# Experts' up projections with one 512-column moving operand, and most of the choice's one-hot sets under the experts

## The reference, cut to what matters

```python
def expert_choice_moe(h, lp):
    b, t, dm = h.shape
    cap = EC_CAPACITY * t // N_EXPERTS                      # 256
    affinity = jax.nn.softmax((h @ lp['router']).astype(jnp.float32), axis=-1)
    gate, idx = lax.top_k(jnp.swapaxes(affinity, 1, 2), cap)
    xs = jax.vmap(lambda hb, ib: hb[ib])(h, idx)
    hid = (jax.nn.silu(jnp.einsum('becd,edf->becf', xs, lp['moe_w1']))
           * jnp.einsum('becd,edf->becf', xs, lp['moe_w3']))
    y = jnp.einsum('becf,efd->becd', hid, lp['moe_w2']) * gate[..., None].astype(h.dtype)
    return jax.vmap(lambda yb, ib: jnp.zeros((t, dm), y.dtype).at[ib.reshape(-1)].add(yb.reshape(-1, dm)))(y, idx)
```

## Time and profile before

| | us |
|---|---|
| median of 3 runs | 4239.88 (4237.48 to 4244.39) |
| the profiled execution, its own time | 4230.22 |
| its span | 4228.4 |
| mean granted clock of TensorE, share of full | 0.935 |

### The profile page before, as it was taken

How to read it: one execution, slowest core, us unless ns; L and a number is a source line. 1 busy time by engine, 2 the same in 40 slices (tenths; PEclk the granted TensorE clock), 3 DMA queues, 4 the chain that set the end, 5 groups by cost and what they waited for, 6 DMA issues and landing times. The chain is left out here.

```text
span 4228.4 us, 114308 instructions
## 1 busy us (share of the span) xinstructions
PE 3605.5 (85%) x50045; PEld 3209.7 (76%) x50045; DVE 2429.1 (57%) x4363; ACT 1873.2 (44%) x3274; POOL 1295.8 (31%) x1262
## 2 busy tenths in 40 slices
PE   5799999999677777777777588798299999999997
PEld 2678888888577777777777588675199999999987
DVE  3246676620057676667766655433856666666666
ACT  3246665531145555555555544233044444444454
POOL 2223333321155555555554145101110201010202
PEclk8899999999889999999999889898599999999999
DMA  5235555532333333333332367342156767676787
GB/s 176 66 124 178 180 179 172 171 120 72 103 81 85 87 91 80 88 89 80 93 86 62 122 179 229 104 159 100 61 185 199 217 201 218 201 215 204 223 289 224
DMA packets 565269, 612.66 MB, mean 145 GB/s; under 512 B 66018, under 2 KB 469284, under 8 KB 563748
## 3 DMA queue, kind: packets, MB, share of 16 engines
q1 hardware_dynamic: 515620, 493.82, 37.9%
q0 software_dynamic: 22688, 80.75, 6.5%
q10 hardware_dynamic: 26464, 30.77, 2.4%
HBM read 443.62 MB, written 161.50 MB: 143 GB/s over the span
## 5 line engine op out<-in xcount | busy, mean ns | idle before, releaser
L424 DVE TENSOR_TENSOR moe_w_lo<-moe_w_lo_whole,moe_w_hi 128x2048 fp32r<-128x2048 f32 x254 | 446.6, 1758 | 281.7 <-ACT moe_w_hi L625 195.6
L559 PE MATMUL moe_h<-moe_xt_hi,moe_w_hi 128*128 128x256 f32 x2048 | 583.2, 285 | 6.6 <-DVE moe_w_lo L424 3.3
L559 PE MATMUL moe_h<-moe_xt_lo,moe_w_hi 128*128 128x256 f32 x2048 | 580.6, 283 | 0.0
L559 PE MATMUL moe_h<-moe_xt_hi,moe_w_lo 128*128 128x256 f32 x2048 | 580.5, 283 | 0.0
L1878 PE MATMUL inward_pp<-u_u_hi,inward_w_hi 128*128 128x512 f32 (+1 forms) x1360 | 527.1, 388 | 19.9 <-POOL inward_w_lo L2038 19.9
L1878 PE MATMUL inward_pp<-u_u_lo,inward_w_hi 128*128 128x512 f32 (+1 forms) x1360 | 515.5, 379 | 0.0
L1878 PE MATMUL inward_pp<-u_u_hi,inward_w_lo 128*128 128x512 f32 (+1 forms) x1360 | 515.3, 379 | 0.0
L559 PEld LDWEIGHTS moe_h<-moe_xt_hi,moe_w_hi 128*128 128x128 f32 x2048 | 393.7, 192 | 20.3 <-DVE moe_w_lo L424 8.8
L559 PEld LDWEIGHTS moe_h<-moe_xt_lo,moe_w_hi 128*128 128x128 f32 x2048 | 393.8, 192 | 3.6
L559 PEld LDWEIGHTS moe_h<-moe_xt_hi,moe_w_lo 128*128 128x128 f32 x2048 | 393.8, 192 | 0.0
L481 POOL DMA_INDIRECT scratch_x<-moe_ys,moe_who x30 | 88.2, 2941 | 843.9 <-DVE moe_ys L710 727.0
(11 more groups left out here) (395 smaller groups left out, 9868.7 us busy)
## 6 DMA issues: line engine op xcount, KB each, us to landing
moe_w_lo_whole<-in_moe_w SPq DMA_DIRECT2D x384, 512.0 KB, 5.4
scratch_ops<-inward_ops SPq DMA_DIRECT2D x72, 514.0 KB, 3.8
scan_over<-scratch_ops SPq DMA_DIRECT2D x72, 512.0 KB, 10.1
inward_w_lo_whole<-in_w_in SPq DMA_DIRECT2D x38, 512.0 KB, 4.6
scan_aq<-scratch_ops SPq DMA_DIRECT2D x36, 516.0 KB, 5.2
scratch_gates<-inward_out SPq DMA_DIRECT2D x64, 256.0 KB, 2.1
all_late<-in_w_mod POOLq DMA_DIRECT2D x32, 512.0 KB, 4.7
rest_modsum<-scratch_gates SPq DMA_DIRECT2D x64, 256.0 KB, 3.9
```

The costliest lines, as they stand in the source:

```text
L424: return nc.vector.tensor_tensor(x_lo, x, x_hi.bitcast(F32), ALU.subtract)
L559: mm = nc.tensor.matmul(hb[ft % 2][m][:, 0:CAP], w_, x_, start=(k == 0 and part == 0), stop=(k == KD - 1 and part == 2))
```

## The change

1. The experts' rows lie upper part and rest beside each other (`xt_parts`), so that one matmul of 512 columns with the same weights does upper by upper into the first half of a PSUM bank and upper by rest into the second half; rest by upper stays a matmul of 256 columns into the first half. Per slice 32 matmuls in place of 48.
2. The halves are added by VectorE: two `tensor_reduce` over pairs that lie 256 elements apart (steps hs0 and hs1), out of PSUM into `sl` and `hid`. Silu waits for hs0 and works in place in SBUF; `hid` then multiplies in SBUF. TensorE's `turn` waits for hs1.
3. In `choose` only the one-hot sets of experts 0 to 2 are left (`EARLY` = 3). The first weights' rests and the first rows' rests go from GpSimd to VectorE. The transposes of the first rows come after set 1.
4. The sets 3 to 15 are made in `experts`: expert e makes set e + 3 in slices 1 to 6 (3, 3, 3, 3, 2 and 2 tiles), at the end of VectorE's part of the slice. TensorE multiplies set e + 2 in slice 0 of expert e (1 to 13) between the first two `h` (`rows_of`), into bank `yb[0]`, after q3 of the expert before. VectorE collects it at the end of slice 0, and `down(0)` waits for that. GpSimd takes token numbers from `idxf`.
5. The tiles of `choose` share memory with the final norm's ring `x`.

```diff
-            pool.wait_ge(s_hi, 2)
-            pool.tensor_tensor(w13_lo[:, 0], w13[:, 0], w13_hi[:, 0].bitcast(F32), ALU.subtract).then_inc(s_lo, 1)
-            pool.tensor_tensor(w2_lo[:, 0], w2[:, 0], w2_hi[:, 0].bitcast(F32), ALU.subtract).then_inc(s_lo, 1)
...
-            for e in range(E_NUM):
+            def compare(e):
                 if e >= 2:
                     dve.wait_ge(s_mm, e - 1)
                 for k in range(NT):
                     at = (k // 2) * E_NUM + e
                     ins = dve.tensor_scalar(oh[:, e % 2, k, :], slots[:, :], slot[:, k % 2, at:at + 1], None, ALU.is_equal)
                 ins.then_inc(s_oh, 1)
-                if e:
-                    collect(e - 1)
-            collect(E_NUM - 1)
...
+            compare(0)
+            dve.wait_ge(s_hi, 2)
+            dve.tensor_tensor(w13_lo[:, 0], w13[:, 0], w13_hi[:, 0].bitcast(F32), ALU.subtract).then_inc(s_lo, 1)
+            collect(0)
+            compare(1)
+            dve.tensor_tensor(w2_lo[:, 0], w2[:, 0], w2_hi[:, 0].bitcast(F32), ALU.subtract).then_inc(s_lo, 1)
+            compare(2)
+            collect(1)
+            for q in range(4):
+                lower_rows(q)
+            collect(2)
...
-        xt, xt_lo = n.sb_both("xt_lo", [P, 2, KD, CAP])
-        xt_hi = n.sb("xt_hi", [P, 2, KD, CAP], F32R)
+        xt_whole, xt_part = n.sb_both("xt_parts", [P, 2, KD, 2, CAP])
+        xt, xt_hi, xt_lo = xt_whole[:, :, :, 1, :], xt_part[:, :, :, 0, :], xt_part[:, :, :, 1, :]
...
+        COMPARE = {1: range(0, 3), 2: range(3, 6), 3: range(6, 9), 4: range(9, 12), 5: range(12, 14), 6: range(14, 16)}
...
                         if ft == 0:
-
                             DV.wait(pe, f"{w}q3", j) if u else None
+                            if 1 <= 2 * i + u <= E_NUM - EARLY:
+                                pe.wait_ge(s_out, 2 * (2 * i + u))
...
+                    def rows_of(e):
+                        pe.wait_ge(s_oh, e - EARLY + 1)
+                        DV.wait(pe, f"{w}q3", j)
+                        for h in range(2):
+                            for k in range(NT):
+                                mm = nc.tensor.matmul(yb[0][:, 5 * h:5 * h + 5], oh[:, e % 2, k, h * P:(h + 1) * P], parts[:, k, e, :],
+                                                      start=(k == 0), stop=(k == NT - 1))
+                        mm.then_inc(s_listed, 1)
...
-                                xhi, xlo = xt_hi[:, u, k, :], xt_lo[:, u, k, :]
-                                for part, (w_, x_) in enumerate(((whi, xhi), (whi, xlo), (wlo, xhi))):
-                                    mm = nc.tensor.matmul(hb[ft % 2][m][:, 0:CAP], w_, x_, start=(k == 0 and part == 0),
-                                                          stop=(k == KD - 1 and part == 2))
+                                both = xt_part[:, u, k, :, :].rearrange("p a c -> p (a c)")
+                                if k == 0:
+                                    nc.tensor.matmul(hb[ft % 2][m][:, :], whi, both, start=True, stop=False)
+                                mm = nc.tensor.matmul(hb[ft % 2][m][:, 0:CAP], wlo, xt_hi[:, u, k, :], start=False, stop=False)
+                                if k:
+                                    mm = nc.tensor.matmul(hb[ft % 2][m][:, :], whi, both, start=False, stop=(k == KD - 1))
...
-                                DV.wait(pe, f"{u}hid{FT - 2 + part}", i)
+                                DV.wait(pe, f"{u}hs1{FT - 2 + part}", i)
                                 PE.did(f"{u}x{part}", turn(1 - u, part))
                         if ft:
                             down(ft - 1)
+                        elif 1 <= 2 * i + u <= E_NUM - EARLY:
+                            rows_of(2 * i + u + EARLY - 1)
...
-                        PE.wait(act, f"{u}h{ft}", i)
-
-                        DV.wait(act, f"{u}hid{ft - 2}" if ft >= 2 else f"{w}hid{ft + 6}", i if ft >= 2 else j)
-                        ins = act.activation(sl[:, ft % 2, :], hb[ft % 2][0][:, 0:CAP], ACT.Silu)
+                        DV.wait(act, f"{u}hs0{ft}", i)
+                        ins = act.activation(sl[:, ft % 2, :], sl[:, ft % 2, :], ACT.Silu)
...
+                        PE.wait(dve, f"{u}h{ft}", i)
+                        PE.wait(dve, f"{u}y{ft - 2}" if ft >= 2 else f"{w}y{ft + 6}", i if ft >= 2 else j)
+                        for m, to_ in enumerate((sl[:, ft % 2, :], whole)):
+                            ins = dve.tensor_reduce(to_, hb[ft % 2][m][:, :].rearrange("p (a c) -> p c a", a=2), AX_X, ALU.add)
...
+                        if ft == 0 and 1 <= e <= E_NUM - EARLY:
+                            collect(e + EARLY - 1)
+                        if ft in COMPARE and e < E_NUM - EARLY:
+                            compare(e + EARLY, COMPARE[ft])
```

117 lines of the change are left out of this document (66 added, 51 removed).

## The result

| | before | after |
|---|---|---|
| median of the comparison's 4 runs each, us | 4241.46 | 4207.35 (4197.89 to 4211.94) |
| the profiled execution, its own time, us | 4230.22 | 4211.72 |
| its span, us | 4228.4 | 4209.9 |

The ratio of the times is 0.9923, 95% interval 0.9907 to 0.994. The forecast was 4203.4 us, a gain of 36.5; the medians moved by 34.1. The profiled execution of after lies 4 us above its own median.

What follows compares the result with a forecast made beforehand. TensorE was taken to bound the experts, with VectorE's chain setting its start at an expert's end. Terms -42.4 - 17.3 + 11.7 + 12.4 - 2.9 + 2.0 = -36.5 us gave 4203.4 us, range 4190 to 4229.

Steps and rivals of the forecast that it cites:

- The choice, -36.2 and -6.2: Ahead of the experts: first set to first h falls from 59.6 to 23.4 us; GpSimd's subtractions leaving the search save 6.2.
- wrong if it comes after 3030: Sign at the experts' start: first h expected about 3026.5 us; after 3030 would mean slower gather or modulation.
- 512 columns, -17.3: In the h matmuls of 13 experts: 10.4 ns less per k and bank, 0.166 us per slice, -17.3 us.
- Rival 2: In the h matmuls: 512 columns win 2.6 ns or nothing, not 10.4; 4216 to 4221 us, chance 0.07.
- The sets, +11.7: On TensorE under the experts: 13 moved one-hot sets' matmuls at 0.9 us each, without waits, +11.7 us.
- The reductions: On VectorE, pairs 1 KB apart in PSUM: 0.68 us each taken, between bounds of 0.68 and 1.23 us.
- Rival 1: On VectorE: the strided reduction costs 1.23 us, adding 1.1 us at each expert's end; 4221 us, chance 0.26.
- The expert's end, +0.95: At each expert's end: VectorE's chain and the next h come 0.95 us later, +12.4 us over 13 experts.
- The last three experts, +2.0: In the last experts: no sets, savings and delays mostly drown in DMA time; 0 to +5, taken as +2 us.
- inside a slice the reductions cost nothing: Within an expert's slices: VectorE's idle stretches, such as 2.22 us waiting for ScalarE, cover the reductions; no cost.
- Rival 3: In every slice: VectorE becomes the bound, slower overall if a reduction reaches 1.56 us; 4302 us at 1.8, chance 0.05.
- Rival 4: In every expert: an unseen wait of 1.5 to 2.5 us where VectorE's lag meets TensorE; 4227 to 4243 us, chance 0.09.

Runs made afterwards that it cites:

- e1: The changed kernel run once more, unaltered, for a second trace: 4198.8 us, ratio 0.9913 to the kernel before.
- e11: After with first collect ahead of w1/w3 rest, ScalarE casting all next rows' upper parts, 256 columns without reductions in the last three experts: 4184.11 us, 0.9878 of before.
- e10: After with first collect ahead of w1/w3 rest, ScalarE casting all next rows' upper parts, 256 columns and no reductions in any expert: 4195.16 us, 0.9905 of before.
- e5: The changed kernel with each reduction done twice, the second into a tile nothing reads: 4230.8 us, 0.9995 of before.
- e3: The kernel before with only the 512-column matmuls and the two reductions added, choice unchanged: 4234.72 us, 1.0005 of before.
- e2: The changed kernel with three 256-column h products as before and no reductions, moved choice kept: 4196.15 us, 0.9915 of before.

## Why the prediction came out right, and where its steps did not

**The choice, -36.2 and -6.2: right.** The stretch from the search to `h` shortened by 41.6 us (e1 43.1), predicted 42.4. Its path term by term: set 0 and the rest of w1 and w3 5.3 us to the collect (5.6 predicted), second gather issue at 7.65 (7.8), first transposes at 14.30 (12.9), modulation's start to end 6.4 (6.8), first `h` at 24.16 (23.4). The one miss is the landing, 6.65 us from issue to transposes in after where the earlier trace rows gave 5.1. In the eleven traces of the new choice it is 5.1 to 5.5 us in seven and 6.3 to 6.8 in four. So one row gave the more frequent price and hid the spread. It is nearly all that differs between these stretches: from the first transposes to the first `h` they all take 9.8 to 9.9 us. The first `h` came at 3039.43 and not near 3026.5, and by the prediction's own sign (wrong if it comes after 3030) this would speak against it. That test was badly made. It counted from the span's start, and so held 12.1 us of upstream chance, without which it is 3027.3; the distance from the search's start is the test.

**512 columns, -17.3: right in size, 10.4 ns as read.** A pair is 3183.84 - 3183.50 = 0.34 us, and an `h` 5.59 us over 16, 349 ns, as the sum of 229.2 and 119.8 had it. With its reductions this half is worth 14.5 us in e11 against e10 over the 13 experts, where they cost 0.35 us at each transposes. Rival 2 falls. The Trainium skill's figures ("TensorE: Matmul & The Clock Gate", section "Back-to-back issue gap") would have the pair at 325.0 ns; here it is 349, and the rows of before stood closer. That section of the Trainium skill gives them as the gap of a single, isolated matmul, which the prediction did not say. The `down` also became quicker by 0.03 us a slice, 0.2 an expert, which I had not in the sum and can't explain.

**The sets, +11.7: 0.82 us each, +10.7.** No wait before them and none for their collect, as argued. They run in experts 1 to 13, so the prediction's "No sets" for the last three was wrong by one.

**The reductions: 0.68 to 0.69 us, the lower bound.** Rival 1, to which I gave 0.26, falls. The 128 rows of each kind above lie within 20 ns. The Trainium skill ("Advanced Engine Details and Errata", section "Memory Cachelines") asks in PSUM that every two consecutive elements be contiguous, for best throughput. VectorE here reads pairs 1 KB apart at the rate of a plain read, so for this access no penalty shows, while the SBUF penalty of the earlier trace rows stands.

**The expert's end, +0.95: right as a sum, split differently.** Transposes +0.45 (TensorE waits 0.51 for hs1, the row at 3175.47) and `down` to `h` +0.52, together 0.97. I had put the wait for hs1 under cover ("`down(7)` still ends earlier than x1"), and it is covered here: the two waits together are one delay of x1, seen in two places. With the reductions doubled (e5) the whole delay stands at the transposes. The second `h`'s wait: -0.22 predicted, -0.26 seen (11.91 to 11.33 less 0.32 of faster `h`).

**The period: 71.0 predicted, 70.7 measured**, from the `down` (0.2) and the set (0.1). Over the stretch up to expert 12 the experts lose about 1 us in place of the 3.9 of my sum. VectorE is 83% busy. The prediction wrote 85, but its own terms, 48.3 + 16 x 0.68 = 59.2 us of 71.0, give 83.

**The last three experts, +2.0: the mis-sized term.** They measured +10.0 (239.5 to 249.5 us). I looked there for shared DMA time and VectorE's load ("savings and delays both drown mostly in DMA time"), and took the reductions as a push of a few us. The step that failed is "inside a slice the reductions cost nothing": it was argued from a slice in which ScalarE has the upper part of the weights ready early. Where that part is late, behind a transfer or behind the final norm's work on ScalarE, `w13l` comes late on VectorE, and the change puts Silu behind it, where it had run beside it. The longest wait, 4.48 us, falls where the DMA engines are idle (4024.7 to 4029.3, share 0.00). The earlier trace rows show 30 us of shared DMA time, and the prediction read all three experts by them. e3 shows the loss without the moved choice, e2, e10 and e11 its absence without the reductions. In the pair of traces before and after, longer waits make 7.0 us of it, the lower clock 5.8 and one set 0.8, less 3.8 for the quicker `h`. What share belongs to the scales is not settled.

**Why the total was still near.** Terms by which I was off: last experts +8, sets -1, `down` and rest -2, choice +0.8. The medians' -34.1 against -36.5 is closer than these would give: they sum to +6, and from the search on the traces gain 30.6 us. The stages ahead vary by more than the difference. The mechanism of the gain was right; that the total came within 2.4 us is partly luck, since the term missed by 8 us was met by others with the opposite sign.

**Rivals 3 and 4.** Rival 3's decision at X = 1.56 was not reached, and e5 at 1.37 shows no middle slice stretched. Rival 4, an unseen wait of 1.5 to 2.5 us in every expert, is not there; its mechanism, a lag of VectorE that meets TensorE, exists in three experts.
